# One step of global attention on TensorE put in another order, its maxima taken three steps ahead from queries read in order

## The chip, the cores and the metric

The kernel runs on one core of one Trainium2 chip. The metric is the device time of one execution in microseconds (us), as the median of several runs. Times inside an execution are read from the profile of one of them, counted from the start of its span.

## What is computed

The reference is one encoder layer in float32 on x of 2048 tokens by 1024: RMS norm, a projection to the heads of two attention groups, global attention (group A), windowed attention (group B), an output projection, and a feed-forward part. The change lies in the global attention alone:

```
def global_axial_gqa(q, k, v, gq, gk):          # 8 query heads, 2 key heads, head size 64
    q, k = axial_rope(rmsnorm(q, gq)), axial_rope(rmsnorm(k, gk))
    ...
    s = jnp.einsum('bkgqd,bksd->bkgqs', qblk, k) * HEAD_DIM ** -0.5
    p = jax.nn.softmax(s, axis=-1)
    return jnp.einsum('bkgqs,bksd->bkgqd', p, v)
```

## The kernel before

Five stages run one after another: `project`, `attend_global`, `attend_window`, `mix_heads`, `ffn`. All arithmetic is float32, made of parts in the format fp32r (a high and a low part), which TensorE takes at one pass a product.

`attend_global` works through TOTAL = 32 blocks n, each of 512 queries (QB) of one head against all 2048 keys. A block has UNITS = 8 units u of 256 keys. For each unit:

- TensorE, `scores(n, u)`: four products of 512 columns into one of two halves of `s_ps`. Lines 741 and 742 stand once for each of two 128-key tiles. The second of each pair has 65 rows: 64 of the low parts of the keys, and one row of ones against row 64 of `q_max`, in which the negated maximum of each query lies. So a score comes out with its maximum subtracted already.
- ScalarE, `exponentials`: exp into `p_hi` (fp32r, line 658) and exp again in place in `s_ps` (line 659).
- VectorE, `low`: `p_lo` is the difference of the two (line 695).
- TensorE, `weigh`: two products of values with `p_hi` into `oa_ps`, two with `p_lo` into `ob_ps`. It runs LAG = 2 units behind the scores.
- GpSimd: it adds `p_hi` of the units up in `p_sum` (line 626, seven adds of 128x1024 a block, the first for unit 1), folds the two halves at the block's end (line 630), and after the add of unit 4 joins the output of the block before, `combine` (lines 612 and 616), which signals `summed`. `p_hi` has four slots, so ScalarE may be at most four units ahead of GpSimd's adds.

The maxima of a later block come from products of their own. `max_products` makes two products of 128 queries by 512 keys into `m_ps` (line 724), with the queries as weights; VectorE reduces them (`reduce`, line 679). A block has PAIRS = 8 such pairs, one in each unit, and `pair_of` says which: in unit u it is pair (u + EARLY) mod 8 of block n + 1, or of n + 2 in the last EARLY units. With EARLY = 2 the last pair of block n + 1 falls in unit 5 of block n. Then VectorE takes the maxima together (line 683), negates them into `neg_max` (line 686) and signals `max_ready`.

SyncE's queue, `place_max` (line 552), copies `neg_max` into row 64 of `q_max`. `neg_max` has its queries across the 128 partitions, four to a partition, and the row has 512 in a line. The queries of a group t are taken with step 4 (`t::QT`), so that the four maxima of a partition lie beside each other in the row: one transfer of 128 pieces of 16 bytes. `scores(n + 1, 0)` waits for it (`max_placed`).

The queue's order for block n is written out by hand: `load_q(n + 3)`, `shift(n - 1)`, `store(n - 1)`, `place_max(n + 1)`. Each is a wait followed by one or more transfers. `store(n - 1)` waits for `summed`, that is for GpSimd's `combine(n - 1)`; so `place_max(n + 1)` stands behind it too.

TensorE's order in a unit is `scores`, `weigh`, `max_products`, and after unit 4's also `total`, the product of the block before's sums with ones.

Of the kernel before, what the change touches and what calls it, by code (L numbers as in the profile page):

```python
# [21 lines left out]
F32 = mybir.dt.float32  # L22
# [5 lines left out]
P = 128  # L28
# [3 lines left out]
HD = 64  # L32
# [22 lines left out]
def at_least(eng, sem, value):  # L55

    if isinstance(value, int) and value <= 0:
        return
    eng.wait_ge(sem, value)
# [410 lines left out]
def attend_global(nc, a, scratch):  # L470
    ITER = GRP * (SEQ // QB)
    TOTAL = NG * ITER
    UNITS = NT // 2
# [3 lines left out]
    LAG = 2  # L477
    SLOTS = 4
    QS = 4
    EARLY = 2  # L480
    ADDS = UNITS
    ONE_LOW, ONE_HIGH = HD, HD + 32
    with ExitStack() as ctx:
# [52 lines left out]
        @block.sync  # L536
        def _(sp):
            def load_q(n):
                at_least(sp, scores_ready, UNITS * (n - QS + 1))
                sp.dma_start(q_all[:, n % QS].bitcast(F32), q_chunks[n // HC, n % HC]).then_inc(q_loaded[n % QS], 16)  # L540
                sp.dma_start(q_max[0:HD, n % QS].bitcast(F32), q_chunks[n // HC, n % HC, HD:2 * HD]).then_inc(q_loaded[n % QS], 16)

            def load_k(g):
                for half in (slice(0, HD), slice(HD, 2 * HD)):
                    sp.dma_start(kt[half, g, 0].bitcast(F32), scratch["k_t"][g, 0:HD]).then_inc(k_loaded[g], 16)

            def load_k_low(g):
                sp.dma_start(kt[0:HD, g, 1].bitcast(F32), scratch["k_t"][g, HD:2 * HD]).then_inc(k_low_loaded[g], 16)

            def place_max(n):  # L550
                sp.wait_ge(max_ready, n + 1)
                sp.dma_start(q_max[HD:HD + 1, n % QS].bitcast(F32).rearrange("o (p t) -> o p t", t=QT), neg_max[:, n % 2].bitcast(F32)).then_inc(max_placed[n % 2], 16)

            def shift(n):
                s = n % 2
                sp.wait_ge(oa_kept, n + 1)
                at_least(sp, summed, n - 1)
                sp.dma_start(o_down[0:HD, s], o_a[HD:2 * HD, s]).then_inc(shifted[s], 16)
                sp.wait_ge(ob_kept, n + 1)
                sp.dma_start(scratch["den"][0, n:n + 1], o_b[ONE_LOW:ONE_LOW + 1, s]).then_inc(den_stored[s], 16)  # L560
                if n > 0:
                    sp.dma_start(scratch["den"][1, n - 1:n], o_b[ONE_HIGH:ONE_HIGH + 1, s]).then_inc(den_stored[s], 16)

            def store(n):
                s = n % 2
                sp.wait_ge(summed, n + 1)
                sp.dma_start(o_chunks[n // HC, n % HC], o_sum[0:HD, s]).then_inc(o_stored[s], 16)

            load_q(0)
            load_k(0)  # L570
            load_q(1)
            load_k_low(0)
            sp.dma_start(v[:].bitcast(F32), scratch["v_glob"].rearrange("t p g c -> p t g c")).then_inc(v_loaded, 16)
            for g in range(NG):
                sp.dma_start(v_one[:, :, g, 0:HD].bitcast(F32), scratch["v_glob"][:, :, g, 0:HD].rearrange("t p c -> p t c")).then_inc(v_loaded, 16)
            load_q(2)
            for g in range(1, NG):
                load_k(g)
                load_k_low(g)
            place_max(0)  # L580
            for n in range(TOTAL):
                if n + 3 < TOTAL:
                    load_q(n + 3)
                if n > 0:
                    shift(n - 1)
                    store(n - 1)
                if n + 1 < TOTAL:
                    place_max(n + 1)
            shift(TOTAL - 1)
            store(TOTAL - 1)  # L590
            sp.wait_ge(ob_kept, TOTAL + 1)
            sp.dma_start(scratch["den"][1, TOTAL - 1:TOTAL], o_b[ONE_HIGH:ONE_HIGH + 1, TOTAL % 2]).then_inc(den_stored[TOTAL % 2], 16)
            for s in range(2):
                sp.wait_ge(o_stored[s], 16 * (TOTAL // 2))
                sp.wait_ge(den_stored[s], 32 * (TOTAL // 2))
# [78 lines left out]
        @block.vector  # L674
        def _(dve):
            def reduce(n, m):
                products = first_bank(m) if n == 0 else m_ps[:]
                dve.wait_ge(max_product, PAIRS * n + m + 1)
                nc.vector.tensor_reduce(part_max[:, m // (PAIRS // QT), m % (PAIRS // QT):m % (PAIRS // QT) + 1],  # L679
                                        products.rearrange("p b c -> p (b c)"), AX, ALU.max).then_inc(max_reduced, 1)  # L680
                if m == PAIRS - 1:
                    nc.vector.drain()
                    nc.vector.tensor_reduce(row_max[:], part_max[:], AX, ALU.max)
                    nc.vector.drain()
                    at_least(dve, max_placed[n % 2], 16 * (n // 2))
                    nc.vector.tensor_scalar(neg_max[:, n % 2], row_max[:], -1.0, None, ALU.mult).then_inc(max_ready, 1)

            def low(n, u):
                at = UNITS * n + u
                slot = at % SLOTS  # L690
                scored = s_ps[:, 2 * (u % 2):2 * (u % 2) + 2].rearrange("p b c -> p (b c)")
                dve.wait_ge(p_hi_ready, at + 1)
                dve.wait_ge(probs_ready, at + 1)
                at_least(dve, low_used, at - SLOTS + 1)
                nc.vector.tensor_tensor(p_lo[:, slot], scored, p_hi[:, slot].bitcast(F32), ALU.subtract).then_inc(p_lo_ready, 1)  # L695

            for m in range(PAIRS):
                reduce(0, m)
            for m in range(EARLY):
                reduce(1, m)  # L700
            for n in range(TOTAL):
                for u in range(UNITS):
                    if n > 0 or u > 0:
                        low(n if u else n - 1, (u - 1) % UNITS)
                    ahead, m = pair_of(n, u)
                    if ahead < TOTAL:
                        reduce(ahead, m)
            low(TOTAL - 1, UNITS - 1)

        @block.tensor  # L710
        def _(pe):
            def max_products(n, m):
                bank = first_bank(m) if n == 0 else m_ps
                t, c = m // (PAIRS // QT), 2 * (m % (PAIRS // QT))
                pe.wait_ge(q_loaded[n % QS], 32 * (n // QS + 1))
                pe.wait_ge(k_loaded[n // ITER], 32)
                if n == 0:
                    at_least(pe, max_reduced, m - 2)
                elif n == 1 and m == 0:
                    pe.wait_ge(max_reduced, PAIRS)  # L720
                else:
                    pe.wait_ge(max_reduced, PAIRS * n + m)
                for e in range(2):
                    last = nc.tensor.matmul(bank[:, e], q_all[:, n % QS, t::QT],  # L724
                                            kt[:, n // ITER, 0, (c + e) * NB:(c + e + 1) * NB], start=True, stop=True)
                last.then_inc(max_product, 1)

            def scores(n, u):
                at = UNITS * n + u
                g = n // ITER  # L730
                if u == 0:
                    pe.wait_ge(max_placed[n % 2], 16 * (n // 2 + 1))
                    pe.wait_ge(k_low_loaded[g], 16)
                if n == 0 and u < 2:
                    pe.wait_ge(filled, 1)
                    pe.wait_ge(max_reduced, PAIRS)
                at_least(pe, p_lo_ready, at - 1)
                for e in range(2):
                    keys = slice((2 * u + e) * P, (2 * u + e + 1) * P)
                    bank = s_ps[:, 2 * (u % 2) + e]  # L740
                    nc.tensor.matmul(bank, kt[:, g, 0, keys], q_all[:, n % QS], start=True, stop=False)  # L741
                    last = nc.tensor.matmul(bank, kt[0:HD + 1, g, 1, keys], q_max[0:HD + 1, n % QS], start=False, stop=True)  # L742
                last.then_inc(scores_ready, 1)
# [30 lines left out]
            for n in range(TOTAL):  # L774
                for u in range(UNITS):
                    at = UNITS * n + u
                    scores(n, u)
                    if at >= LAG:
                        weigh((at - LAG) // UNITS, (at - LAG) % UNITS)
                    ahead, m = pair_of(n, u)  # L780
                    if ahead < TOTAL:
                        max_products(ahead, m)
                    if u == 4 and n > 0:
                        total(n - 1, False)
            for u in range(UNITS - LAG, UNITS):
# [1083 lines left out]
```

## Time and profile before

| | |
|---|---|
| time, median of 3 runs | 3029.72 us (3029.05 to 3031.0) |
| the profiled execution | 3032.3 us, of which its span 3030.7 us |
| global attention, first to last score product | 373.8 to 1076 us |
| mean granted TensorE clock | 0.973 of 2.4 GHz |

The span of the profile goes from the first to the last instruction. An engine's busy time is the sum of its instructions'. In rows of the timeline the first number is the start, the second the duration, and what stands in brackets is how long the engine sat idle before, and what ended that.

### The profile page before, as it was taken

How to read it: one execution, taken by the hardware profiler on the slowest of the kernel's cores; microseconds unless marked ns; L12 is line 12 of the kernel's file. 1: busy time of each engine (PE TensorE's matmuls, PEld its weight loads, DVE VectorE, ACT ScalarE, POOL GpSimd, SP SyncE). 2: the span in 40 equal slices, each digit the busy share in tenths (PEclk: the TensorE clock that was granted, in tenths of full speed). 3: DMA queues.
4: the chain of work that ended last, by engine and by line, in shares of the span. 5: the costliest groups of instructions: out<-in, count | busy, mean ns of one | idle time of the engine just before them, and what ended most of it. 6: DMA issues, size and time to landing. Idle time of an engine off the chain costs nothing. (4 is left out here: it accounts for less than half of the span.)

```text
span 3030.7 us, 38875 instructions
## 1 busy us (share of the span) xinstructions
PE 2827.5 (93%) x12978; PEld 2318.1 (76%) x12978; DVE 1659.6 (55%) x2193; ACT 1329.4 (44%) x1882; POOL 910.1 (30%) x683
## 2 busy tenths in 40 slices
PE   7999499999999969979969999999999999999998
PEld 5888377777777738958858888888888888888887
DVE  5666388888888838855534432354224542254322
ACT  3222177777777738953323322244223432233221
POOL 1221189999999945532200000000001000010000
PEclk9999699999999979989979999999999999999999
DMA  5333611111111022348873343343434343343432
GB/s 174 107 107 98 159 25 32 30 29 34 27 34 29 18 78 79 83 139 206 235 215 98 97 147 90 110 134 97 151 90 134 109 125 118 93 151 97 122 94 83
DMA packets 473643, 308.96 MB, mean 102 GB/s; under 512 B 62451, under 2 KB 440579, under 8 KB 473148
## 3 DMA queue, kind: packets, MB, share of 16 engines
q1 hardware_dynamic: 443484, 274.46, 32.2%
q0 software_dynamic: 6496, 19.42, 2.0%
q10 hardware_dynamic: 23552, 13.64, 1.5%
q8 instruction: 65, 1.06, 0.2%
q14 instruction: 46, 0.38, 0.0%
HBM read 236.79 MB, written 66.40 MB: 100 GB/s over the span
## 5 line engine op out<-in xcount | busy, mean ns | idle before, releaser
L1686 DVE TENSOR_TENSOR f_w_lo<-f_w_raw,f_w_hi 128x1024 fp32r<-128x1024 f32 x256 | 313.8, 1226 | 864.3 <-ACT f_w_hi L1638 864.1
L1638 ACT ACTIVATE f_w_hi<-f_w_raw 128x1024 fp32r<-128x1024 f32 x256 | 271.4, 1060 | 980.4 <-PE f_down L122 553.1
L626 POOL TENSOR_TENSOR p_sum<-p_sum,p_hi 128x1024 f32<-128x1024 f32 x192 | 458.9, 2390 | 33.1 <-issue 25.1
L120 PE MATMUL f_up<-f_h,f_w_hi 128*128 128x512 f32 x1024 | 400.9, 391 | 19.7 <-DMA f_h<-h_split 19.7
L120 PE MATMUL f_down<-f_act_hi,f_w_hi 128*128 128x512 f32 x1024 | 401.2, 392 | 0.0
L122 PE MATMUL f_up<-f_h,f_w_lo 128*128 128x512 f32 x1024 | 399.8, 390 | 0.0
L121 PE MATMUL f_up<-f_h,f_w_hi 128*128 128x512 f32 x1024 | 399.8, 390 | 0.0
L122 PE MATMUL f_down<-f_act_hi,f_w_lo 128*128 128x512 f32 x1024 | 398.8, 389 | 0.0
L121 PE MATMUL f_down<-f_act_lo,f_w_hi 128*128 128x512 f32 x1024 | 398.3, 389 | 0.0
L679 DVE TENSOR_REDUCE part_max<-m_ps 128x1 f32<-128x1024 f32 x251 | 306.8, 1222 | 116.9 <-PE m_ps L724 116.9
L1614 POOL TENSOR_TENSOR f_rstd<-f_var,f_half 128x4 f32<-128x4 f32 x4 | 5.1, 1285 | 1186.3 <-DVE f_var L1706 1186.3
L658 ACT ACTIVATE p_hi<-s_ps 128x1024 fp32r<-128x1024 f32 x256 | 263.6, 1030 | 219.3 <-PE s_ps L742 219.3
L695 DVE TENSOR_TENSOR p_lo<-s_ps,p_hi 128x1024 fp32r<-128x1024 f32 x256 | 310.5, 1213 | 11.6 <-ACT s_ps L659 9.4
L741 PE MATMUL s_ps<-q_all,kt 128*128 128x512 f32 x512 | 226.9, 443 | 48.4 <-DVE p_lo L695 30.3
L659 ACT ACTIVATE s_ps<-s_ps 128x1024 f32<-128x1024 f32 x256 | 262.2, 1024 | 0.0
L120 PEld LDWEIGHTS f_up<-f_h,f_w_hi 128*128 128x128 f32 x1024 | 193.0, 189 | 61.5 <-issue 17.5
L122 PEld LDWEIGHTS f_up<-f_h,f_w_lo 128*128 128x128 f32 x1024 | 193.0, 189 | 40.6
L121 PEld LDWEIGHTS f_up<-f_h,f_w_hi 128*128 128x128 f32 x1024 | 193.2, 189 | 39.8
L122 PEld LDWEIGHTS f_down<-f_act_hi,f_w_lo 128*128 128x128 f32 x1024 | 192.2, 188 | 40.5
L121 PEld LDWEIGHTS f_down<-f_act_lo,f_w_hi 128*128 128x128 f32 x1024 | 192.3, 188 | 39.4
L120 PEld LDWEIGHTS f_down<-f_act_hi,f_w_hi 128*128 128x128 f32 x1024 | 192.2, 188 | 38.8
L742 PE MATMUL s_ps<-q_max,kt 65*128 65x512 f32 x512 | 204.6, 400 | 0.0
(202 smaller groups left out, 4841.3 us busy)
## 6 DMA issues: line engine op xcount, KB each, us to landing
f_w_raw<-in_w_ffn_up SPq DMA_DIRECT2D x128, 512.0 KB, 4.1
f_w_raw<-in_w_ffn_down SPq DMA_DIRECT2D x128, 512.0 KB, 3.8
f_h<-h_split SPq DMA_DIRECT2D x32, 512.0 KB, 5.7
x_in<-in_x SPq DMA_DIRECT2D x16, 512.0 KB, 4.2
q_split<-q_out ACTq DMA_DIRECT2D x16, 512.0 KB, 3.3
q_turned<-w_raw SPq DMA_DIRECT2D x16, 512.0 KB, 3.4
q_all<-q_turned SPq DMA_DIRECT2D x32, 256.0 KB, 3.3
wq_in<-q_split SPq DMA_DIRECT2D x32, 256.0 KB, 2.8
```

Of the source, the lines that this page charges most:

```text
L120: nc.tensor.matmul(out, stat_hi, mov_hi, start=first, stop=False)
L121: nc.tensor.matmul(out, stat_hi, mov_lo, start=False, stop=False)
L122: return nc.tensor.matmul(out, stat_lo, mov_hi, start=False, stop=last)
L626: nc.gpsimd.tensor_tensor(p_sum[:, s], first, p_hi[:, (UNITS * n + u) % SLOTS].bitcast(F32), ALU.add).then_inc(added, 1)
L658: nc.scalar.activation(p_hi[:, slot], scored, ACT.Exp).then_inc(p_hi_ready, 1)
L659: nc.scalar.activation(scored, scored, ACT.Exp).then_inc(probs_ready, 1)
L679: nc.vector.tensor_reduce(part_max[:, m // (PAIRS // QT), m % (PAIRS // QT):m % (PAIRS // QT) + 1], products.rearrange("p b c -> p (b c)") ...
L695: nc.vector.tensor_tensor(p_lo[:, slot], scored, p_hi[:, slot].bitcast(F32), ALU.subtract).then_inc(p_lo_ready, 1)
L741: nc.tensor.matmul(bank, kt[:, g, 0, keys], q_all[:, n % QS], start=True, stop=False)
L742: last = nc.tensor.matmul(bank, kt[0:HD + 1, g, 1, keys], q_max[0:HD + 1, n % QS], start=False, stop=True)
L1638: nc.scalar.activation(w_hi[:, s], w_raw[:, s], ACT.Copy).then_inc(w_hi_made, 1)
L1686: nc.vector.tensor_tensor(w_lo[:, s], w_raw[:, s], w_hi[:, s].bitcast(F32), ALU.subtract).then_inc(w_lo_made, 1)
```

## The change

Three things change in `attend_global`:

- In each unit TensorE issues `max_products` before `weigh`, not behind it.
- EARLY is 3. The last pair of block n + 1 falls in unit 4 of block n, and three pairs of block 1 are made before the first scores.
- The queries of a group are 128 neighbours (`t * P:(t + 1) * P`), so the weights of line 724 are read in order. The maxima of one group then lie in a line of the row, and those of one partition lie 128 apart: `place_max` becomes four transfers, each of 128 pieces of 4 bytes. The counts on `max_placed` grow by the factor four.

The adds on GpSimd, the lines of ScalarE and VectorE's own work stay as they are.

```
-    EARLY = 2
+    EARLY = 3
...
             def place_max(n):
                 sp.wait_ge(max_ready, n + 1)
-                sp.dma_start(q_max[HD:HD + 1, n % QS].bitcast(F32).rearrange("o (p t) -> o p t", t=QT), neg_max[:, n % 2].bitcast(F32)).then_inc(max_placed[n % 2], 16)
+                for t in range(QT):
+                    row = q_max[HD:HD + 1, n % QS, t * P:(t + 1) * P].bitcast(F32)
+                    sp.dma_start(row.unsqueeze(2), neg_max[:, n % 2, t:t + 1].bitcast(F32)).then_inc(max_placed[n % 2], 16)
...
-                    at_least(dve, max_placed[n % 2], 16 * (n // 2))
+                    at_least(dve, max_placed[n % 2], 16 * QT * (n // 2))
...
-                    last = nc.tensor.matmul(bank[:, e], q_all[:, n % QS, t::QT],
+                    last = nc.tensor.matmul(bank[:, e], q_all[:, n % QS, t * P:(t + 1) * P],
...
-                    pe.wait_ge(max_placed[n % 2], 16 * (n // 2 + 1))
+                    pe.wait_ge(max_placed[n % 2], 16 * QT * (n // 2 + 1))
...
                     scores(n, u)
-                    if at >= LAG:
-                        weigh((at - LAG) // UNITS, (at - LAG) % UNITS)
                     ahead, m = pair_of(n, u)
                     if ahead < TOTAL:
                         max_products(ahead, m)
+                    if at >= LAG:
+                        weigh((at - LAG) // UNITS, (at - LAG) % UNITS)
```

## Rows read from the trace of the kernel before

**Rows 1.** The page: engines' busy time, share of the span, instructions.

```profile
PE 2827.5 (93%) x12978; PEld 2318.1 (76%) x12978; DVE 1659.6 (55%) x2193; ACT 1329.4 (44%) x1882; POOL 910.1 (30%) x683
```

**Rows 2.** Windows, 500 to 700 us: busy PE, PEld, DVE, ACT, POOL; clock, DMA.

```profile
500.00:700.00 200.00, 186.90 (x747) 146.06 (x746) 174.93 (x164) 149.62 (x164) 186.75 (x92) 1.00 0.13 31
```

**Rows 3.** Groups by shape, 372 to 1076 us: busy, mean ns, idle before, releaser.

```profile
L679 DVE TENSOR_REDUCE part_max<-m_ps 128x1 f32<-128x1024 f32 x246 | 300.7, 1222 | 91.1 <-PE m_ps L724 91.1
...
L724 PEld LDWEIGHTS m_ps<-kt,q_all 128*128 128x128 f32 x492 | 133.7, 309 | 11.3 <-issue 0.4
...
L741 PEld LDWEIGHTS s_ps<-q_all,kt 128*128 128x128 f32 x512 | 97.5, 190 | 102.1 <-DVE p_lo L695 68.6 <-issue 19.0
```

**Rows 4.** Timeline, 700 to 724 us, one block: start, duration, engine.

```profile
700.34 1.28 POOL L616 TENSOR_TENSOR o_sum<-o_half,o_b 64x512 f32<-64x512 f32 x1
...
701.15 0.49 DVE L686 TENSOR_SCALAR neg_max<-row_max 128x4 fp32r<-128x4 f32 x1
...
701.56 1.21 DVE L695 TENSOR_TENSOR p_lo<-s_ps,p_hi 128x1024 fp32r<-128x1024 f32 x1
701.64 0.49 SPq L567 DMA_DIRECT2D o_turned<-o_sum  x1
701.78 2.36 POOL L626 TENSOR_TENSOR p_sum<-p_sum,p_hi 128x1024 f32<-128x1024 f32 x1 [0.16 <-ACT p_hi L658]
702.18 0.60 SPq L552 DMA_DIRECT2D q_max<-neg_max  x1
...
705.25 0.40 PE L741 MATMUL s_ps<-q_all,kt 128*128 128x512 f32 x1
...
706.38 1.03 ACT L658 ACTIVATE p_hi<-s_ps 128x1024 fp32r<-128x1024 f32 x1 [0.38 <-PE s_ps L742]
...
709.10 1.03 ACT L658 ACTIVATE p_hi<-s_ps 128x1024 fp32r<-128x1024 f32 x1 [0.77 <-PE s_ps L742]
...
710.97 0.59 ACT L640 ACTIVATE o_a<-oa_ps 128x512 f32<-128x512 f32 x1
...
711.92 1.04 ACT L658 ACTIVATE p_hi<-s_ps 128x1024 fp32r<-128x1024 f32 x1
...
713.48 2.39 POOL L626 TENSOR_TENSOR p_sum<-p_sum,p_hi 128x1024 f32<-128x1024 f32 x1 [0.16 <-issue]
...
722.35 1.29 POOL L616 TENSOR_TENSOR o_sum<-o_half,o_b 64x512 f32<-64x512 f32 x1
```

**Rows 5.** Timeline of GpSimd: line 616 as run in blocks 1 and 31.

```profile
413.85 1.28 POOL L616 TENSOR_TENSOR o_sum<-o_half,o_b 64x512 f32<-64x512 f32 x1
...
1074.89 1.29 POOL L616 TENSOR_TENSOR o_sum<-o_half,o_b 64x512 f32<-64x512 f32 x1
```

**Rows 6.** The tile `neg_max`, 500 to 700 us: its transfer, minimum, median, maximum.

```profile
L552 SPq DMA_DIRECT2D q_max<-neg_max x9: 596/596/597, 503.9 to 680.1; - x9
...
DMA to landing us min/median/max: 2.0/2.1/2.1
```

**Rows 7.** Timeline of block 0: an add and `neg_max`.

```profile
391.12 2.39 POOL L626 TENSOR_TENSOR p_sum<-p_sum,p_hi 128x1024 f32<-128x1024 f32 x1 [0.16 <-issue]
...
392.72 0.82 DVE L686 TENSOR_SCALAR neg_max<-row_max 128x4 fp32r<-128x4 f32 x1
```

**Rows 8.** Timeline of the stage's start, SyncE's queue and TensorE.

```profile
338.87 1.22 SPq L545 DMA_DIRECT2D kt<-k_turned  x2
...
363.20 0.70 SPq L552 DMA_DIRECT2D q_max<-neg_max  x1
...
373.80 0.76 PE L741 MATMUL s_ps<-q_all,kt 128*128 128x512 f32 x1 [10.96 <-issue]
```

**Rows 9.** Timeline of GpSimd: first adds of blocks 0 and 1.

```profile
379.54 2.38 POOL L626 TENSOR_TENSOR p_sum<-p_hi 128x1024 f32<-128x1024 f32 x1 [35.50 <-ACT p_hi L658]
...
402.11 2.38 POOL L626 TENSOR_TENSOR p_sum<-p_hi 128x1024 f32<-128x1024 f32 x1 [1.20 <-ACT p_hi L658]
```

**Rows 10.** Timeline of the stage's end: the last add.

```profile
1081.38 2.34 POOL L626 TENSOR_TENSOR p_sum<-p_sum,p_hi 128x1024 f32<-128x1024 f32 x1 [0.16 <-issue]
```

## The prediction

> **What bounds the kernel now.** The page comes first: TensorE is busy for 93% of the span, GpSimd for 30% [rows 1]. That is a mean over five stages. In the windows of global attention the two are level, 186.9 and 186.75 us of 200, at full clock [rows 2]. What a busy engine leaves idle decides, so I went to GpSimd's own timeline. Behind each instruction it pauses 0.16 us at most, also where another engine is named as releaser [rows 4]: that pause is its own drain. A block by GpSimd is the distance between two ends of line 616: 723.64 - 701.62 = 22.02 us in this pair [rows 4], and over 30 blocks (1076.18 - 415.13) / 30 = 22.035 us [rows 5]. GpSimd has no gap in those 30 blocks that would let them be shorter. It is the bound.
>
> How do the others keep step with it, when they could be faster? ScalarE's four slots would hold it back, but are never full: the add at 713.48 is unit 2's, whose `p_hi` ended at 712.96 [rows 4]. The tie is on VectorE. `neg_max` starts at 701.15 and ends at 701.64, 0.02 us behind line 616's end at 701.62 [rows 4]. In block 0 it starts at 392.72, inside an add that ends at 393.51, and ends at 393.54 [rows 7]. So the little negation can't run until GpSimd's current instruction is through. `p_lo` stands behind it on VectorE, and the scores two units on wait for `p_lo`. TensorE's loop alone would be faster, by the 0.3 us of this stall at least; GpSimd drags it along once a block.
>
> **What the reordering and the earlier maxima remove.** VectorE idles 91.1 us for `m_ps` [rows 3]. Putting two products ahead of four lets it start about 0.9 us sooner in each unit (ten score, weight and maximum products fill 2.33 us on TensorE, so 0.233 us apiece, from the pace of the unbroken stretches in which 186.9 us are busy). All of it falls on engines that wait for GpSimd. Worth 0 while GpSimd has work; without that cover it would be 22.03 less TensorE's own 8 x 2.33 + 1.0 (`total`) = 19.6, or 2.4 us a block. The weights of line 724 take 309 ns, those of 741, read in order, 190 [rows 3]. Loads overlap products: worth 0, and in no case over 16 x 0.12 = 1.9 us a block, which is part of the same hidden 2.4. EARLY = 3 adds one pair ahead of the first scores, 1.2 us on VectorE, in the 10.96 us that TensorE idles before 373.80 [rows 8]: 0.
>
> **What the four placements add.** `place_max(n + 1)` stands in SyncE's queue behind `store(n - 1)`, which waits for line 616. `neg_max` being ready a unit earlier doesn't free it. Call line 616's end T (701.62). The store's issue ends at T + 0.51 and the placement is issued at T + 0.56 [rows 4]. One issue takes 0.596 us in nine of nine, and landing is 2.0 to 2.1 us from the issue's start [rows 6]. Back-to-back issues elsewhere: two in 1.22 us [rows 8], so 0.61 each and up to 0.05 between. I take 0.65 a step, since each piece is an element's transfer as before and the count of pieces (128) is the same; bounds 0.50 (a store's issue) and 0.75 (the 0.70 in a crowded queue and 0.05 [rows 8]). The fourth lands at
>
> T + 0.56 + 3 x 0.65 + 2.05 = T + 4.56 (bounds T + 4.1 and T + 4.9). Now it is T + 2.6, and the scores start at 705.25 = T + 3.63 for want of TensorE [rows 4]: hidden by 1.0 us.
>
> Here stands the Trainium skill's page "DMA: Bandwidth & Descriptors", section "Anatomy of one DMA": it gives some 50 ns to the sequencer's dispatch of a transfer and calls descriptor generation small; the section is on transfers that GpSimd issues. By it, as an estimate, the fourth would land at T + 2.8 and nothing would be seen of it. The row's 0.596 speaks against it here.
>
> From the landing L to GpSimd's next need, by rows of block n + 1 [rows 4], as distances:
> - L to the first scores' start, with the extra of a first product after a wait: 0.16. One unit on: 2.33. Scores' start to `p_hi`'s: 706.38 - 705.25 = 1.13. So `p_hi` of unit 1 starts at L + 3.62.
> - ScalarE then keeps the two outputs of the block before (line 640 at 710.97) and comes to unit 2: 711.92 - 709.10 = 2.82. That `p_hi` takes 1.04, and the add starts 0.08 later at best: L + 7.56.
> - The add of unit 2 starts at 713.48 = T + 11.86 in GpSimd's own pace.
>
> The slip is L + 7.56 - 11.86 = 0.26 us with L at 4.56. The add of unit 1, one add (2.39 + 0.16) sooner at T + 9.31, is met (L + 3.62 + 1.11 = 9.29), and from unit 3 on TensorE's 2.33 a unit outruns GpSimd's 2.55. A new loop thus closes through all: line 616, SyncE's queue, four placements, scores, ScalarE, GpSimd's adds of units 2 to 4 and `combine` again, 22.03 + 0.26 = 22.29 us. It has 30 turns: +7.8 us. With the bounds of L: 0 to 0.6 a turn, 0 to +18 us.
>
> What is queued behind the waits: behind `scores(n + 1, 0)` stand on TensorE the maximum products and `weigh` of unit 6 and 7, so VectorE and ScalarE drain too; TensorE waits there for 1 us or more each block. Behind the placements on SyncE stand `load_q` (three blocks ahead) and `shift`, 7 us off: 0. `neg_max` now comes around T + 17.7, inside the add of unit 4, and holds VectorE until that ends, about 2 us (in block 0 it was 0.82 [rows 7]). `p_lo` behind it and the scores of unit 6 are late by a unit, but GpSimd needs that `p_hi` some 2 us later: 0, and it is why TensorE's lead doesn't grow.
>
> **The ends.** From the first add to block 1's takes 402.11 - 379.54 = 22.57 us [rows 9]. GpSimd alone needs 22.03 less `combine`'s two of 1.28 and 0.1: 19.4. Up to 3.2 us is there to win. But the first three adds wait for TensorE's slow start, the same in both orders, and `neg_max` sits in the way a unit sooner. I take 0.8 (bounds 0 and 3.2). The first placement landed 10.4 us after its issue among loads; three small ones behind it add at most 0.3. The last block has neither placements nor maxima; GpSimd ends it in its own pace.
>
> **Sum.** +7.8 - 0.8 = +7.0 us. The profiled execution's 3032.3 would become 3039.3; the median lies 2.6 us below it, so 3036.7; I round to 3036.5.
>
> **The rivals.** "Measurable" is 0.2% here, 6 us, about what can be told from no change.
> - *Placements hidden, GpSimd still the bound.* Issues a little closer (0.55), or the landing at 1.9: L falls under T + 4.3 and the slip is 0. Left: the start's gain. 3026.5 to 3030, likely 3029. For it: 0.26 us is a thin margin on a sum of nine terms. Against: all issues seen behind another took 0.6.
> - *The chain is dearer.* Issues of 128 single elements at 0.75 or more, or landings that queue, or TensorE's clock falling in the pauses: 0.5 us a turn and more, +15 us or more, 3044 upwards. Pauses of 0.9 us on TensorE leave the clock at 1.00 now [rows 2]; those to come are little longer.
> - *Faster.* The order matters on GpSimd after all. At the stage's end, with no maxima and few products about, an add takes 2.34 [rows 10]; in mid-stage 2.39 [rows 4]. If spreading VectorE's work made all 224 adds that short, and the placements stayed hidden, it is -0.05 x 224 = -11 us: 3018. It decides from 2.36 down. Against: the same instructions overlap each add as before, only elsewhere.
> - *TensorE or VectorE is the bound*, and GpSimd's full time chance: -2.4 x 32 = -77 us, 2953. GpSimd's 22 us of work a block forbid it; below 1 in 100.
>
> **Chances.** The slip as forecast 0.48; hidden 0.32; dearer 0.14; shorter adds 0.05; rest 0.01. Within the forecast (3031 to 3043) some three fifths lie over 3035.8, where slower begins. Slower: 0.48 x 0.65 + 0.14 = 0.45. Faster: 0.06. Within 0.2%: 0.49. The range 3027.5 to 3045 leaves out the shorter adds, the far end of the dearer chain, and a little of the hidden case. The likeliest case is the slip, so that is the time given, though it lies close to the border.
>
> **What the profile after would show.** Right: ends of line 616 22.2 to 22.4 us apart; line 552 four times a block, 0.6 to 0.7 apart, the first 0.56 behind line 616's end; TensorE idle about 1 us or more at line 741, released by a transfer; the add of unit 2 waiting some 0.3 us for `p_hi`, all others 0.16; line 724's loads near 190 ns; VectorE's idle time for `m_ps` much smaller; `neg_max` lasting up to 2 us, ending as an add ends. Wrong: a block of 22.03 with no wait of GpSimd (hidden); adds under 2.36 us; or a granted clock below 1.00 in mid-stage.

## The result, and the profile after

| | before | after |
|---|---|---|
| median | 3029.75 us (3028.24 to 3031.53, 9 runs) | 3036.44 us (3034.14 to 3043.23, 9 runs) |
| the profiled execution's span | 3030.7 us | 3034.8 us |
| mean distance of two ends of `combine`, mid-stage | 22.035 us | 22.195 us |

The ratio is 1.0023, with a 95% interval of 1.0014 to 1.0031: slower by 0.2%, close to what was forecast (3036.5). In `after` the lines of `attend_global` stand two lower (679 is 681, 741 is 743, and so on).

The page's line of busy times, and the window from 500 to 700 us, say next to nothing against [rows 1, 2]: VectorE is 8.5 us busier in 200, GpSimd 1.6 us less. The negation accounts for VectorE's part: it lasts 1.64 us in the median and not 0.48, and counts as busy while it is held up.

```profile
PE 2832.2 (93%) x12978; PEld 2278.7 (75%) x12978; DVE 1687.4 (56%) x2193; ACT 1329.5 (44%) x1882; POOL 910.8 (30%) x683
```
```profile
500.00:700.00 200.00, 187.93 (x741) 134.09 (x740) 183.41 (x163) 147.97 (x162) 185.17 (x91) 1.00 0.14 31
```

The groups by shape, 372 to 1080 us (busy, mean ns, idle before, releaser), show what the edit did do [against rows 3]: the weights load in 190 ns and not 309, and VectorE waits 30.2 us for maximum products and not 91.1. Both were won where nobody waits.

```profile
L743 PEld LDWEIGHTS s_ps<-q_all,kt 128*128 128x128 f32 x510 | 97.0, 190 | 117.8 <-DVE p_lo L697 42.5 <-DMA q_max<-neg_max 39.4 <-issue 18.1
...
L681 DVE TENSOR_REDUCE part_max<-m_ps 128x1 f32<-128x1024 f32 x245 | 297.6, 1215 | 30.2 <-PE m_ps L726 30.2
...
L726 PEld LDWEIGHTS m_ps<-kt,q_all 128*128 128x128 f32 x490 | 83.3, 190 | 53.6 <-issue 39.7
```

The first of these lines has a releaser that [rows 3] lack: TensorE waits for a placement in every block from the third on. The timeline of one block, 698 to 726 us, is the counterpart of [rows 4]:

```profile
698.76 2.38 POOL L628 TENSOR_TENSOR p_sum<-p_sum,p_hi 128x1024 f32<-128x1024 f32 x1 [0.16 <-issue]
699.52 1.64 DVE L688 TENSOR_SCALAR neg_max<-row_max 128x4 fp32r<-128x4 f32 x1
...
702.52 1.28 POOL L618 TENSOR_TENSOR o_sum<-o_half,o_b 64x512 f32<-64x512 f32 x1
...
703.83 0.49 SPq L569 DMA_DIRECT2D o_turned<-o_sum  x1
...
704.36 2.53 SPq L554 DMA_DIRECT2D q_max<-neg_max  x4
...
708.37 0.50 PE L743 MATMUL s_ps<-q_all,kt 128*128 128x512 f32 x1 [0.85 <-DMA q_max<-neg_max]
...
711.91 1.03 ACT L660 ACTIVATE p_hi<-s_ps 128x1024 fp32r<-128x1024 f32 x1 [0.37 <-PE s_ps L744]
...
714.73 1.04 ACT L660 ACTIVATE p_hi<-s_ps 128x1024 fp32r<-128x1024 f32 x1
...
715.85 2.40 POOL L628 TENSOR_TENSOR p_sum<-p_sum,p_hi 128x1024 f32<-128x1024 f32 x1 [0.33 <-ACT p_hi L660]
...
724.72 1.28 POOL L618 TENSOR_TENSOR o_sum<-o_half,o_b 64x512 f32<-64x512 f32 x1
```

Read it as a circle. `combine` ends at T = 703.80. Its signal lets SyncE issue the store at 703.83, then the four placements at T + 0.56. TensorE, which has idled for it, starts the block's scores at 708.37 = T + 4.57. The `p_hi` of unit 2 starts at 714.73 and ends at 715.77, and GpSimd, which could have begun at T + 11.86 = 715.66, begins its add at 715.85. From there to the next end of `combine`, at 726.00, GpSimd works without a gap. That is 4.57 + 7.48 + 10.15 = 22.20 us. The negation at 699.52 lies in the add of unit 4 and lasts 1.64 us, until that add is through (701.14); nobody in the circle waits for it.

The turns, from GpSimd's timeline [against rows 5]: the 29 from the first of these rows to block 30's take 22.14 to 22.24 us, 22.195 on average, and the last one 23.31 us, up to the end of the third row.

```profile
414.01 1.28 POOL L618 TENSOR_TENSOR o_sum<-o_half,o_b 64x512 f32<-64x512 f32 x1
...
1057.68 1.28 POOL L618 TENSOR_TENSOR o_sum<-o_half,o_b 64x512 f32<-64x512 f32 x1
...
1081.01 1.26 POOL L618 TENSOR_TENSOR o_sum<-o_half,o_b 64x512 f32<-64x512 f32 x1
```

In that last turn TensorE paused longer ahead of the placement (line 743 idled 2.03 us before 1063.55), as no maximum products are left to make, and then ran at half clock. The windows show it (busy PE, PEld, DVE, ACT, POOL; granted clock 1.00, then 0.53):

```profile
1061.00:1064.00 3.00, 0.97 (x5) 0.49 (x4) 2.24 (x2) 1.58 (x2) 2.84 (x2) 1.00 0.08 1
1064.00:1067.00 3.00, 3.00 (x9) 2.35 (x8) 0.00 (x0) 1.83 (x2) 2.68 (x3) 0.53 0.02 5
```

At the stage's start [against rows 8, 9] the four placements of block 0 are issued from 363.98 in 2.79 us, and the first add comes at 381.50; block 1's comes 20.81 us later, not 22.57. The first scores start at 375.75, 11.77 us behind the issue of the first placement; before it was 373.80 and 10.60. That is no chance of one profile: over all runs of this document the distance is 10.5 to 10.9 us in the six kernels with one placement and 11.4 to 12.1 us in the seven with four.

```profile
381.50 2.39 POOL L628 TENSOR_TENSOR p_sum<-p_hi 128x1024 f32<-128x1024 f32 x1 [36.46 <-ACT p_hi L660]
...
402.31 2.39 POOL L628 TENSOR_TENSOR p_sum<-p_hi 128x1024 f32<-128x1024 f32 x1 [0.78 <-ACT p_hi L660]
```

The books of the two profiled executions: the stage ends 6.1 us later (1093.87 against 1087.76 for the last `combine`). Of these, 1.0 came in with the stage before (its memset starts at 338.83 and not 337.82), -0.85 was won up to the first `combine` (415.29 against 415.13), +4.6 are 29 turns at 0.16, and +1.3 is the turn at half clock (23.31 against 22.00). The later stages, which the edit doesn't touch, were 2.0 us shorter in this one execution.

### The profile page after: what moved, and what is told of

It is laid out like the page before. It is cut to its first block and busy times, and to the rows that moved or that the text cites. A ratio compares the mean times of both kernels' runs of the same rounds, so it can differ in the third digit from the quotient of the medians.

```text
span 3034.8 us, 38971 instructions
## 1 busy us (share of the span) xinstructions
PE 2832.2 (93%) x12978; PEld 2278.7 (75%) x12978; DVE 1687.4 (56%) x2193; ACT 1329.5 (44%) x1882; POOL 910.8 (30%) x683
```

## The experiments

Times in this section stand beside runs of the kernel before on the same chip: medians 3029.69 (e1, e2, e3, e7), 3030.1 (e4, e5, e6, e8) and 3030.27 us (e9, e10, e11). "A block" is the mean distance of ends of `combine` over 30 turns in the profiled execution. The line numbers in the rows differ a little from run to run; the tiles tell what is what.

| run | order, EARLY | placements | negation | adds on GpSimd | a block, us | median, us |
|---|---|---|---|---|---|---|
| before | old, 2 | 1 | own | 7 | 22.035 | 3029.75 |
| after | new, 3 | 4, behind the store | own | 7 | 22.23 | 3036.44 |
| e1 | new, 3 | 4, ahead | own | 7 | 22.02 | 3030.47 |
| e2 | old, 2 | 4, behind | own | 7 | 22.205 | 3037.94 |
| e3 | new, 3 | 1, behind | own | 7 | 22.03 | 3030.06 |
| e7 | new, 3 | 4, behind | in the reduction | 7 | 22.355 | 3048.72 |
| e11 | old, 2 | 1, behind | in the reduction | 7 | 22.03 | 3028.33 |
| e4 | old, 2 | 1, behind | own | 6 | 21.78 | 3020.05 |
| e5 | new, 3 | 4, behind | own | 6 | 22.77 | 3034.52 |
| e6 | new, 3 | 4, ahead | own | 6 | 21.19 | 3002.58 |
| e8 | new, 3 | 4, ahead | in the reduction | 6 | 20.245 | 2973.51 |
| e9 | old, 2 | 1, behind | in the reduction | 6 | 21.77 | 3018.20 |
| e10 | new, 3 | 1, ahead | in the reduction | 6 | 20.535 | 2979.67 |

### The circle cut: placements ahead of the store (e1)

```
                     shift(n - 1)
-                    store(n - 1)
                 if n + 1 < TOTAL:
                     place_max(n + 1)
+                if n > 0:
+                    store(n - 1)
```

> The changed kernel, with the four placements of block n + 1 moved ahead of the store of block n - 1 in SyncE's queue. Nothing else differs. If the lost time is the loop that closes through line 616's successor, the store's wait and the four placements, the loop is cut: ends of combine 22.03 us apart, no add waits for p_hi in mid-stage, TensorE never waits for a placement there, and the time falls by 29 x 0.16 us and the 1.1 us lost in block 31, to about 3030.5 (3029 to 3032). Rival: four transfers, or the new order, cost as such, wherever they stand: 22.2 us a block, 3036.

Measured: 22.02 us a block and 3030.47 us (ratio to before 1.0003, 0.9994 to 1.0012). The loss is gone, by one move in a queue, with the four transfers, the order and the reads all in place. Two ends of `combine`, 30 turns apart:

```profile
412.66 1.28 POOL L619 TENSOR_TENSOR o_sum<-o_half,o_b 64x512 f32<-64x512 f32 x1
...
1073.28 1.26 POOL L619 TENSOR_TENSOR o_sum<-o_half,o_b 64x512 f32<-64x512 f32 x1
```

The list of waits (437 to 1076 us: total, times, longest) now has on top a line that neither the kernel before nor the changed one has. ScalarE waits for GpSimd's adds to free a slot of `p_hi`, so the lead of the other engines is limited by the four slots at last:

```profile
ACT p_hi L661 <- POOL p_sum L629: 96.2, 80, 2.1
```

### The two halves of the change apart (e2, e3)

e2 is the kernel before with the reads in order and four placements alone; e3 has the new order and EARLY = 3 alone (in short form):

```
e2:  -    q_all[:, n % QS, t::QT]            e3:  -    EARLY = 2
     +    q_all[:, n % QS, t * P:(t + 1) * P]     +    EARLY = 3
     +    four transfers in place_max             +    max_products ahead of weigh
```

> The kernel before, with the queries read in order and four placements, but its old order in a unit and EARLY = 2. Here the negation comes in unit 5 and not 4, so it races with the end of combine. Placement loop alone: as in the changed kernel, 22.2 us a block, 3036. But by the rows of before the negation is wanted 17.9 us after the first scores of a block, which now start 4.6 us behind the end of combine T: at T + 22.5 (T + 22.3 without the wait for p_lo in unit 1), 0.1 to 0.3 us behind the next end at T + 22.2. It then meets the add of unit 5 and is held until T + 24.75, the placements are issued 2.1 us later, and the block takes about 24.3 us: 3095 to 3100. I expect this second case (6 in 10). Rival to both: four transfers are free, 22.03 us, 3030.

Measured: 22.205 us a block, 3037.94 us (1.0033, 1.0022 to 1.0044). Four placements, with the reads in order that need them, give the whole loss without the new order; the same reads and the same four transfers are in e1 and cost nothing there. The first of my two cases came out, not the one that I held likelier: the negation escapes GpSimd by a hair. It starts 0.06 us before `combine` ends and is through 0.17 us later, in the pause ahead of the next add at 704.58:

```profile
703.14 1.28 POOL L618 TENSOR_TENSOR o_sum<-o_half,o_b 64x512 f32<-64x512 f32 x1
...
704.36 0.17 DVE L688 TENSOR_SCALAR neg_max<-row_max 128x4 fp32r<-128x4 f32 x1
```

> The kernel before, with the new order in a unit and EARLY = 3, but its queries with step 4 and one placement. The placement lands at T + 2.6, so the scores of a block can start 2 us sooner than with four: no slip. GpSimd the bound: 22.03 us a block, and the start of the stage is passed up to 1 us sooner; 3029 (3027.5 to 3030.5). Rival: the order itself is what costs, 22.2 us and 3036; or the order gains as soon as placements are cheap, below 22.0 us and 3026 or less.

Measured: 22.03 us a block, 3030.06 us (1.0003, 0.9994 to 1.0012). The order and the earlier maxima are worth nothing here, either way. TensorE waits for the single placement too, 1.2 us in nearly every block from 459 us on, and loses nothing by it, as GpSimd never runs out of work; the granted clock stays at 1.00 from 500 to 1000 us.

```profile
679.55 0.50 PE L741 MATMUL s_ps<-q_all,kt 128*128 128x512 f32 x1 [1.22 <-DMA q_max<-neg_max]
```

### Who waits for the negation (e7, e11)

```
-                    nc.vector.tensor_reduce(row_max[:], part_max[:], AX, ALU.max)
-                    nc.vector.drain()
...
-                    nc.vector.tensor_scalar(neg_max[:, n % 2], row_max[:], -1.0, None, ALU.mult).then_inc(max_ready, 1)
+                    nc.vector.tensor_reduce(neg_max[:, n % 2], part_max[:], AX, ALU.max, negate=True).then_inc(max_ready, 1)
+                    nc.vector.drain()
```

e7 is this edit on the changed kernel.

> The changed kernel, with the negation made by the reduction that takes the maxima together, so the separate small instruction between two SBUF tiles is gone. If it is that instruction alone that GpSimd's adds hold up, the 1.6 us in it vanish (the reduction lasts 0.16 us as before) and VectorE's p_lo behind it comes 1.5 us sooner; the loop through the placements doesn't pass there, so still 22.2 us a block and 3036 (3034 to 3038). Rival: VectorE's hold-up is part of the loop, then 22.03 us and 3030.

Measured: 27 turns of about 22.2 us and three of 23.6, and a median of 3048.72 us, out of my range by 10 us. It lies between two pairs of runs: 3039.65 and 3040.98, 3056.45 and 3058.07. That VectorE's hold-up isn't in the circle holds, as the usual turn stayed 22.2. But with it gone TensorE gets further ahead and pauses longer at the placement, 1.67 to 1.75 us in each of 29 blocks and not 0.85, and after three of these pauses its clock falls to about half; these are the three long turns. One of them, in windows and in TensorE's timeline:

```profile
549.00:551.00 2.00, 0.39 (x2) 0.35 (x3) 1.68 (x2) 0.37 (x1) 2.00 (x1) 1.00 0.33 54
551.00:553.00 2.00, 2.00 (x9) 1.64 (x8) 0.67 (x1) 1.14 (x2) 1.84 (x2) 0.85 0.51 152
553.00:555.00 2.00, 2.00 (x6) 1.52 (x6) 1.66 (x2) 0.80 (x1) 1.84 (x2) 0.50 0.00 0
```
```profile
550.61 0.51 PE L742 MATMUL s_ps<-q_all,kt 128*128 128x512 f32 x1 [1.69 <-DMA q_max<-neg_max]
```

The profiled execution is the shortest (3038.1 us span), so what makes the two long ones 17 us longer isn't shown: more such turns, or late placements as in e5 below.

e11 is the same edit on the kernel before.

> The kernel before, with the negation made in the reduction and nothing else. GpSimd stays the bound, 22.03 us a block and 3030 (3028 to 3031.5). What ties TensorE to GpSimd's pace must be another thing then: TensorE runs ahead until the first scores of a block wait for their one placement, which lands 2.6 us behind the end of combine. Rival: no such wait is seen and the end of combine has no fixed distance to the scores.

Measured: 22.03 us a block, 3028.33 us (0.9998, 0.9988 to 1.0007). From 568 us on TensorE waits 0.25 to 0.42 us a block for its single placement (T is 698.14 here, the scores start at T + 2.67 and not at T + 3.63):

```profile
700.81 0.50 PE L740 MATMUL s_ps<-q_all,kt 128*128 128x512 f32 x1 [0.34 <-DMA q_max<-neg_max]
```

So the negation was what tied TensorE to GpSimd in the kernel before. Without it TensorE gets 1.0 us further ahead, and then the placement ties it.

### GpSimd's work cut by one add (e4, e5, e6, e8, e9, e10)

The add of unit 7 goes to TensorE, as two products of `p_hi` with ones, added to the rows that hold the sum of the low parts (the two sums are added later anyway):

```
-                for u in range(1, UNITS):
+                for u in range(1, UNITS - 1):
...
+                if u == UNITS - 1:
+                    for e in range(2):
+                        last = nc.tensor.matmul(ob_ps[:], ones_low[:], p_hi[:, slot, e * QB:(e + 1) * QB], start=False, stop=(e == 1))
                 last.then_inc(low_used, 1)
```

> The kernel before, with the add of unit 7 taken from GpSimd: TensorE sums that p_hi with two products against ones into the rows of the output that hold the low parts' sum, 0.47 us a block. GpSimd then needs 22.03 - 2.55 = 19.5 us a block. If the old order's own loop is close behind GpSimd (21.7 us without the hold-up of the negation), little comes of it: 21.7 to 22.3 us a block, 3020 to 3038. Rival: GpSimd alone was the bound and the order doesn't matter: 20.1 us, 2970.

Measured: 21.78 us a block, 3020.05 us (0.9969, 0.9958 to 0.9980). So the old order has a bound of its own, 0.25 us under GpSimd's 22.035. No run takes it apart: TensorE is busy for 191.9 of the 200 us from 500 on, and GpSimd now waits 27.1 us there for `p_hi`.

> The changed kernel, with the add of unit 7 on TensorE in the same way. The loop through the placements is: end of combine to the first scores 4.57, to the add of unit 2 7.48, to the next end of combine 10.16 = 22.2 us, and the add of unit 7 is not in it. If that loop bounds the changed kernel, taking 2.55 us of work from GpSimd gives nothing: 22.2 us a block, 3036 (3033 to 3039), and GpSimd idles 2.4 us ahead of the add of unit 1. Rival: GpSimd's work is the bound as before and placements only a small addition: 20.1 to 20.5 us a block, 2975.

Measured: 3034.52 us (3033.0 to 3050.49, 12 runs; 1.0015, 1.0006 to 1.0025). GpSimd has 2.55 us less to do a block, and the turns get no shorter; what comes of it are the 2.5 us of the last block (9.10 us and not 11.60). This tells the circle from a plain GpSimd bound more sharply than any other run. In the profiled execution, one of the two long ones (span 3048.0 us), 17 of 30 turns take 22.17 to 22.23 us, as forecast. In such a turn GpSimd idles 2.73 us ahead of the add of unit 1, where 2.4 was expected:

```profile
582.50 2.41 POOL L633 TENSOR_TENSOR p_sum<-p_hi 128x1024 f32<-128x1024 f32 x1 [2.73 <-ACT p_hi L668]
585.27 2.41 POOL L633 TENSOR_TENSOR p_sum<-p_sum,p_hi 128x1024 f32<-128x1024 f32 x1 [0.35 <-ACT p_hi L668]
```

The other thirteen take up to 25.0 us. In ten of them the four issues of the placements took 3.08 to 3.83 us and not 2.53, so the scores start 5.1 to 5.85 us behind T and not 4.57. Six of these ten, at full clock, take 22.8 to 23.4 us; in the other four the clock fell too, and they take 24.3 to 25.0. The three that are left are the first turn, one of 22.49 us, and the last, behind a pause of 2.02 us and at a lower clock. So the circle passes on what a late placement costs. Why an issue takes longer at times isn't shown. Here is one of the four: the issues (T is 617.59), TensorE's pause behind them, and the clock in the windows, which falls to 0.69 in that of the first scores.

```profile
618.16 3.48 SPq L555 DMA_DIRECT2D q_max<-neg_max  x4
```
```profile
623.07 0.50 PE L751 MATMUL s_ps<-q_all,kt 128*128 128x512 f32 x1 [1.77 <-DMA q_max<-neg_max]
```
```profile
620.00:623.00 3.00, 1.29 (x6) 0.75 (x4) 2.42 (x3) 1.91 (x2) 2.68 (x3) 1.00 0.12 6
623.00:626.00 3.00, 2.93 (x9) 2.38 (x10) 1.41 (x2) 1.69 (x2) 1.12 (x1) 0.69 0.48 132
```

> The changed kernel with both: the add of unit 7 on TensorE and the placements ahead of the store. Loop and GpSimd's load are both gone: TensorE needs 8 x 2.33 + 1.0 + 0.47 = 20.1 us a block, GpSimd 19.5, VectorE 19.2 and what the negation is held up, 0 to 2.4. I expect 20.1 to 21.3 us a block, 2971 to 3010, likely 2985. Rival: something else bounds at 22 us, then 3030.

Measured: 21.19 us a block, 3002.58 us (0.9913, 0.9895 to 0.9931), inside the range but above the likely 2985. The tile `neg_max`, 500 to 700 us, shows the negation held up in an add each time, for 1.6 of its 2.4 us in the median (minimum, median, maximum in ns):

```profile
L697 DVE TENSOR_SCALAR neg_max<-row_max x9: 1239/1587/1595, 517.9 to 687.5; 128x4 fp32r<-128x4 f32 x9
```

> The kernel of the run before (sum of unit 7 on TensorE, placements first), with the negation made in the reduction. VectorE's hold-up is gone, TensorE's 20.1 us is the bound: 20.1 to 20.5 us a block, 2970 to 2980. If the hold-up hides behind TensorE anyway, no difference to the run before.

Measured: 20.245 us a block, 2973.51 us (0.9815, 0.9797 to 0.9832): 57 us below the kernel before on the same chip, the fastest here. With GpSimd and the circle out of the way the negation's hold-up costs 0.95 us a block; TensorE is busy all 200 us of the window (busy PE first):

```profile
500.00:700.00 200.00, 200.00 (x831) 153.07 (x830) 187.35 (x169) 162.33 (x179) 179.64 (x90) 1.00 0.15 32
```

> The kernel before, in its old order, with the add of unit 7 on TensorE and the negation made in the reduction. With the add alone moved, the block took 21.78 us and the negation 0.18 us, not held up: the old order's own loop. Taking the negation out of it saves at most its 0.18 us and a drain, so 21.4 to 21.8 us a block, 3008 to 3020. Then the new order is worth the distance to the 20.25 us of the run with all changes. Rival: the order is worth nothing once negation and load are out, 20.3 us and 2975.

Measured: 21.77 us a block, 3018.20 us (0.9960, 0.9946 to 0.9974). The negation costs nothing there. The order, the early maxima, the reads and the queue are together worth 21.77 - 20.245 = 1.5 us a block once GpSimd isn't the bound.

> The kernel with all changes (new order, sum of unit 7 on TensorE, placements first, negation in the reduction), but with queries of step 4 and one placement. TensorE is busy all the time in the one with four. If loading weights at 309 ns against 190 stays hidden even then, 20.25 us a block and 2973.5 (2971 to 2976). Rival: the slower loads show once TensorE is the bound: 16 loads a block, each at most 0.12 us dearer and 0.07 above the pace of a product, 21.3 us at most, 3008.

Measured: 20.535 us a block, 2979.67 us (0.9836, 0.9819 to 0.9852). It lies between my two cases: 0.29 us a block for 16 loads. One placement instead of four is the other difference, but in neither run does TensorE wait for a placement in mid-stage. In its groups the strided loads take 313 ns, and the maximum products behind them 424 ns in the mean, where e8 has 189 and 405:

```profile
L732 PE MATMUL m_ps<-kt,q_all 128*128 128x512 f32 x156 | 53.5, 424 | 0.0
...
L732 PEld LDWEIGHTS m_ps<-kt,q_all 128*128 128x128 f32 x156 | 42.6, 313 | 8.9 <-issue 6.1
```

## Why the prediction was right, point by point

- **GpSimd bounds the kernel before: right.** Three quite different kernels keep the block at 22.02 to 22.03 us (e1, e3, e11), and with one add less the kernel before gets faster (e4), if only by 0.25 us a block.
- **Reordering, early maxima and reads in order are worth nothing: right** (e3), while GpSimd is the bound. The cover's price was put at 2.4 us a block (19.6 against 22.03). With one add moved TensorE needs 0.47 more; by that sum 20.1, measured 20.245 (e8). But e8 also has the queue and the negation changed. Of the way from 22.035 down to there the order, the maxima, the reads and the queue are worth 1.5 us (e9 against e8).
- **The four placements close a circle through `combine`: right,** shown from three sides. Cut, it is gone (e1); in the old order the placements make it too (e2); and less work for GpSimd outside the circle doesn't shorten it (e5). The Trainium skill's page "DMA: Bandwidth & Descriptors", section "Anatomy of one DMA", puts the dispatch of a transfer at some 50 ns; it speaks of transfers that GpSimd issues, and by it the four placements would have been hidden. In SyncE's queue the four issues took 2.53 us, 0.60 each and 0.64 from one to the next, so the trace does not agree for this queue.
- **The terms.** A step in the queue: 0.64 for 0.65. The scores: T + 4.57, for a landing forecast at T + 4.56. The `p_hi` of unit 1: T + 8.11 for 8.18, so the landing, the start behind it and the extra of the first product came to 0.07 less than I had summed. The add of unit 2: T + 12.05 for 12.12. From there to the next end of `combine`: 10.15 for 10.17. Slip: forecast 0.26, measured 22.195 - 22.035 = 0.16 a turn. That makes 4.6 us in 29 turns, for 7.8 forecast in 30.
- **The start: right only in sum** (-0.85 for -0.8). Three small placements behind the first were to add at most 0.3 us; the first scores came 1.17 us later behind that issue (11.77 for 10.60), and the first add 0.95 us later than the stage's own shift. From there to block 1's first add 1.76 us were won (22.57 - 20.81), inside the bounds of 0 to 3.2 but twice the 0.8. Two misses cancel here.
- **TensorE's clock.** I had set it down under the dearer case, for each turn. Behind a pause at the placement it fell once, in block 31, and cost 1.3 us.
- **So the closeness of the time is in part chance.** The stage's books hold 4.6 + 1.3 - 0.85, about +5.1 us, for the +7.0 forecast: a smaller slip, and a slow turn that the forecast lacks. The medians differ by 6.7 us, and the 1.6 between aren't in this profile, whose other stages differ by -1.0 us in all. The longer single runs of the changed kernel (up to 3043.23) may have more slow turns or late placements; no profile of one of them was taken.
- **The negation in the add of unit 4,** about 2 us and no price: 1.64 us, no price (e7's usual turns). That removing it could do harm, by a longer pause of TensorE, I had not seen.

## What to carry to other kernels

An engine with no gap in its timeline, whatever its share on the page, is the bound, and a reorder elsewhere buys nothing until its work is cut. Before you split one small transfer into several, ask what stands ahead of it in its queue: if that waits for the bounding engine, the queue's issue times enter a circle with it. Here it was enough to move the small transfers ahead of the store (e1). Then cut the bound, the circle and the held-up instruction together. In the kernel before, one add less gave 10 us, the negation alone nothing, and both 12. On the changed kernel the queue alone won back 6 us, one add less 2, and the negation alone cost 12. All three with the new order gave 57 us.

## What the runs showed of the hardware

- A 128x4 negation on VectorE from one SBUF tile to another doesn't get through while GpSimd's add is under way. It took 0.17 us in a pause; held up, 0.8 to 1.9 us in an add (e1, e3, e6, the changed kernel) and 0.48 us in `combine` (before), it ended at most 0.04 us behind GpSimd's instruction. The reduction that writes the same four values took 0.16 us, in the midst of an add (e7, e8) or of `combine` (e11). The Trainium skill's page "SBUF — State Buffer", section "Who interferes with whom", calls the pair of ports that VectorE shares with GpSimd an exclusive lock, which a `tensor_scalar` such as this negation can contend for and a reduction on this chip never does. The trace agrees.
- TensorE's granted clock fell to about half after some pauses of 1.7 to 2.1 us at the placement and not after others: after three of 29 in e7, after four in e5's mid-stage, and after the one of 2.03 us in the changed kernel. It stayed at 1.00 after all those of 0.85 us in the changed kernel's mid-stage and those of 1.2 us in e3's. A pause that is no loss in itself can cost in the turn behind it: 1.3 us in the changed kernel, 1.4 in e7, and in e5 some 1.55 beyond what the late scores cost (24.68 - 22.20 - 0.92 in the turn shown).
- Weights read with a step of 16 bytes load in 309 to 313 ns against 189. Behind a stream of products that cost nothing until TensorE had no gap, then 0.29 us for 16 loads.
- SyncE issues four transfers of 128 pieces of 4 bytes 0.64 us apart, where one of 128 pieces of 16 bytes takes 0.60 us: the count of transfers decided, not their bytes. Each landed 2.0 to 2.1 us after its issue. In two profiled executions (e5, e8) some of these issues took up to 1.5 and 1.7 us, and the landing up to 3.0 and 3.1; in before, after, e1, e2, e3, e6 and e7 none was over 0.61 us from 500 to 700 us. What lengthens them isn't shown.
